# The square root of the pre-norm: a first guess by ACT's logarithm and exponential and one Newton step on DVE, for an integer guess and three steps

## The chip, the cores and the metric

The kernel runs on one core of a Trainium2 chip. The metric is the device time of one execution in microseconds (us); the time of before is the median of three runs. TensorE is called PE in the rows, VectorE DVE, ScalarE ACT, GpSimd POOL and SyncE SP.

## The reference

One inference step of a two-layer decoder, for a prompt of 512 tokens and 8 samples of 4 tokens each (544 tokens in all, 1024 features). Each layer has three sublayers, so there are six: feed-forward, mixer, feed-forward, twice. The mixer of the first layer is attention with a short convolution (A/B), that of the second a gated delta rule (C). Every sublayer starts with a norm of its input:

```python
def rmsnorm(x, g):
    xf = x.astype(jnp.float32)
    y = xf * lax.rsqrt(jnp.mean(xf * xf, axis=-1, keepdims=True) + NORM_EPS)
    return (y * g.astype(jnp.float32)).astype(x.dtype)

def swiglu(x, w_gate, w_up, w_down):
    return (jax.nn.silu(x @ w_gate) * (x @ w_up)) @ w_down

for layer in range(DEPTH):
    x = x + 0.5 * rmsnorm(swiglu(rmsnorm(x, gains[0]), ...), gains[1])
    x = x + rmsnorm(mixer(rmsnorm(x, gains[2]), ...), gains[3])
    x = x + 0.5 * rmsnorm(swiglu(rmsnorm(x, gains[4]), ...), gains[5])
```

## The kernel before

Activations lie with features on the partitions and the 544 tokens in columns, in two halves of 272. Every product is made in three passes: weights and activations are each split into a high and a low part, and high by high, high by low and low by high are summed. A **unit** is one block of weights, 128 output features by 1024 (or 1408) inputs, and costs TensorE 48 (or 66) matmuls. For each unit SP loads the raw weights (w_raw, a ring of four), ACT casts them to the high part (w_hi, L440, `act_split`), DVE subtracts to get the low part (w_lo, L447, `dve_split`), and TensorE multiplies (L455 or L467). w_hi and w_lo have two places each, so the cast for unit n + 2 waits until unit n is done.

Each engine has its own program, written out by hand; semaphores alone order them. There is no scheduler: what stands earlier in an engine's code runs earlier.

The norm ahead of a sublayer is folded behind its products. The products run on gain * x, and each result is multiplied by one factor per token, 1 / sqrt(mean + eps), when it is taken from PSUM. TensorE sums the squares over the features in the head of the sublayer (`pe_head`, L481), together with the first two units. DVE (`dve_rstd_x`, L843) writes the mean to a scratch tile, makes the low part of the third unit, and then takes the root into rb, which is called rstd_rows in the rows. `dve_rsqrt` does it by an integer guess of two operations and three Newton steps of three operations, each waiting for the last. Only then can DVE evict the first result, and only behind that eviction does it make the low part of the fourth unit:

```python
            if opening and j == 0:
                dve_rstd_x(e, s, n + 2)
            e.wait_ge(sem("unit_done"), i * 4 + (n + 1))
            if j % 2 == 0:
                e.tensor_tensor(halves(scr[:, m % 2, :]), cols(4 * (m % 2)), halves(rb[:, :]), ...
```

`dve_rsqrt` is also used for the norms behind the sublayers (on 3 columns) and inside mixer C; these stay. The six roots meant here belong to gate_up00, the A/B mixer, gate_up01, gate_up10, the C mixer and gate_up11, in this order. In mixer C, DVE waits for constants that POOL makes (L1746, the last) before it uses the root.

ACT's functions come from tables that are loaded in sets. Before, ACT loads the set with Silu at the head of each gate_up and of mixer C, and the set with logarithm and exponential at the head of mixer A/B and later in mixer C. Copies and squares run with either set.

Of the kernel before, what the change touches and what calls it, by code (L numbers as in the profile page):

```python
# [103 lines left out]
def build(nc, io, subs=SUBLAYERS):  # L104

    stack = ExitStack()
    with stack:
        sems = {}

        def sem(name):  # L110
            if name not in sems:
                sems[name] = stack.enter_context(nc.semaphore(name))
            return sems[name]
# [229 lines left out]
        gemms = {}  # L343
# [49 lines left out]
        def nk_of(n):  # L393
            for name in order:
                g = gemms[name]
                if g["n0"] <= n < g["end"]:
                    return g["nk"]
            return 0
# [33 lines left out]
        def act_split(e, n, i, nk):  # L432

            if not nk:
                return
            e.wait_ge(sem(f"w_raw{n % RAW}"), i * 16 + 16 * (n // RAW + 1))
            if n >= 2:

                e.wait_ge(sem("unit_done"), i * 4 + (n - 1))
            e.copy(w_hi[:, n % 2, 0:nk * P], raw[:, n % RAW, 0:nk * P]).then_inc(sem("w_hi_ready"), 1)  # L440
# [78 lines left out]
        def quads(e, g, body, peel):  # L519

            n = g["quads"] - (1 if peel else 0)
            with e.Fori(0, n) as i:
                body(i, False)
            if peel:
                body(g["quads"] - 1, True)
# [22 lines left out]
            with e.Fori(1, g["quads"]) as i:  # L548
                body(i, 0)

        def act_gate_up(e, g):
            m0 = gate_up_count(g)
            e.preload_act_table(ACT.Silu)

            def body(i, last):
                for j in range(4):
                    n = g["first"] + j
                    act_split(e, n + 2, i, nk_of(n + 2 + 4 * (g["quads"] - 1)) if last else KD)
                    if j % 2:
                        m = m0 + j // 2  # L560
                        e.wait_ge(sem("gate_scaled"), i * 2 + (m + 1))
                        e.activation(scr[:, m % 2, :], scr[:, m % 2, :], ACT.Silu).then_inc(sem("silu_ready"), 1)
                        e.wait_ge(sem("hidden_ready"), PRIMED + i * 2 + (m + 1))
                        e.copy(h_hi[:, bass.ds(i * 2 + j // 2, 1), :],  # L564
                               scr[:, 2 + m % 2:3 + m % 2, :]).then_inc(sem("h_hi_ready"), 1)

            quads(e, g, body, True)

        def dve_gate_up(e, g, s):
            m0 = gate_up_count(g)  # L570
# [158 lines left out]
        def act_y(e, g, y, s, pre):  # L729
            per, n_end = per_quad(g), g["first"] + 4 * (g["quads"] - 1)  # L730
            name = g["name"]

            def whole(i, j):
                n = g["first"] + j
                act_split(e, n + 2, i, g["nk"])
                if per == 4 or j % 2:
                    t = j // 2 if per == 2 else j
                    e.wait_ge(sem("unit_done"), i * 4 + (n + 1))
                    e.copy(y[:, bass.ds(i * per + t, 1), :].rearrange("p o (h t) -> p (o h) t", h=2), cols(2 * (t % 2)))
                    if isinstance(i, int) and i == 0 and t == 0:  # L740
                        to = scr[:, 2, :]
                    else:
                        to = scr[:, t % 2, :]
                        if not (isinstance(i, int) and i * per + t < 3):
                            e.wait_ge(sem("y_accumulated"), i * per + (acc_base[name] + t - 2))
                    e.activation(halves(to), cols(2 * (t % 2)), ACT.Square).then_inc(sem("y_squared"), 1)

            def tail(h):
                for m in tails_of(g):
                    if h == 0 and m >= 3 and per == 2:  # L750
                        e.wait_ge(sem("y_accumulated"), acc_base[name] + m - 2)
                    if h == 0 and per == 4:
                        e.wait_ge(sem("y_accumulated"), acc_base[name] + min(m - 2, KD - 3))
                    bank = 2 * (m % 2) + h
                    e.activation(scr[:, m % 2, half(h)], ps[:, bank, 0:TH], ACT.Square).then_inc(sem("y_squared"), 1)
                for m in tails_of(g):
                    ins = e.copy(y[:, m, half(h)], ps[:, 2 * (m % 2) + h, 0:TH])
                ins.then_inc(sem("tail_out"), 1)

            for j in range(4):  # L760
                whole(0, j)
            if g["quads"] > 2:
                with e.Fori(1, g["quads"] - 1) as i:
                    for j in range(4):
                        whole(i, j)
            for j in range(2):
                whole(g["quads"] - 1, j)
            e.wait_ge(sem("tail_done"), s + 1)
            tail(0)
            act_split(e, n_end + 4, 0, nk_of(n_end + 4))  # L770
            if pre:
                act_pre(e, s + 1, 0, 0, 2)
            e.wait_ge(sem("unit_done"), n_end + 4)
            tail(1)
            act_split(e, n_end + 5, 0, nk_of(n_end + 5))
            if pre:
                act_pre(e, s + 1, 0, 2, KD)
                act_pre(e, s + 1, 1, 0, KD)
# [41 lines left out]
        def dve_rsqrt(e, out, tmp, x):  # L820

            chain(e, e.tensor_scalar(tmp.bitcast(I32), x.bitcast(I32), 1, None, ALU.arith_shift_right))
            chain(e, e.tensor_scalar(out.bitcast(I32), tmp.bitcast(I32), -1, MAGIC, ALU.mult, ALU.add))
            for _ in range(3):
                chain(e, e.tensor_tensor(tmp, out, out, ALU.mult))
                chain(e, e.scalar_tensor_tensor(tmp, tmp, -0.5, x, ALU.mult, ALU.mult))
                chain(e, e.scalar_tensor_tensor(out, tmp, 1.5, out, ALU.add, ALU.mult))
# [15 lines left out]
        def dve_rstd_x(e, s, n):  # L843

            e.wait_ge(sem("squares_summed"), 2 * KD * (s + 1))
            mean, tmp = scr[:, 2, :], scr[:, 3, :]
            e.tensor_scalar(halves(mean), cols(4), 1.0 / D_MODEL, EPS, ALU.mult, ALU.add).then_inc(sem("mean_ready"), 1)
            dve_split(e, n, 0, KD)
            e.wait_ge(sem("mean_ready"), s + 1)
            dve_rsqrt(e, rb[:, :], tmp, mean)  # L850

        def gain(l, n, k):
            at = (l * 6 + n) * KD + k
# [501 lines left out]
        def act_ab(e, at):  # L1355
            g = gemms["ab_qkv"]
            e.preload_act_table_set("natural_log_exp_and_others")
            act_split(e, g["n0"] + 2, 0, KD)
            for u in range(11):
                act_split(e, g["first"] + u + 2, 0, KD)  # L1360
                if u == 1:
                    e.wait_ge(sem("vector_stage"), nth["gate_abs"])
                    e.activation(scr[0:A_HEADS, 1, :], scr[0:A_HEADS, 1, :], ACT.Exp
                                 ).then_inc(sem("scalar_stage"), reached("gate_exp"))
                if u == 2:
                    e.wait_ge(sem("vector_stage"), nth["gate_exp1"])
                    e.activation(scr[0:A_HEADS, 3, :], scr[0:A_HEADS, 2, :], ACT.Ln
                                 ).then_inc(sem("scalar_stage"), reached("gate_log"))
# [879 lines left out]
            return ext(m)[:, CP:CW].rearrange("p (b t) -> p b t", t=CS)  # L2248

        def act_c(e, at):  # L2250
            e.preload_act_table(ACT.Silu)

            g = gemms["c_qkv"]

            def raw_out(i, j):
# [26 lines left out]
                        silu_out(i, j - 1)  # L2282

            act_split(e, g["n0"] + 2, 0, KD)
            body(0, True, False)
            with e.Fori(1, g["quads"] - 1) as i:
                body(i, False, False)
# [564 lines left out]
        @block.scalar  # L2852
        def _(e):
            act_split(e, 0, 0, KD)
            e.wait_ge(sem("vector_stage"), nth["gains_ready"])
            act_pre(e, 0, 0, 0, KD)
            act_split(e, 1, 0, KD)
            act_pre(e, 0, 1, 0, KD)
            for s, (kind, l, w) in enumerate(subs):
                if kind == "ffn":  # L2860
                    act_gate_up(e, gemms[f"gate_up{l}{w}"])
                    act_y(e, gemms[f"down{l}{w}"], y_ffn, s, s + 1 < len(subs))
                if kind == "ab":
                    act_ab(e, s)
                if kind == "c":
                    act_c(e, s)
            for u in (0, 1, 2, 3, 4, 6):
                e.wait_ge(sem("rows_psum"), u + 1)
                e.copy(rows_p[:, u // 2, 4 * (u % 2) * P:4 * (u % 2 + 1) * P], ps[:, u % 4, :]).then_inc(sem("rows_out"), 1)
            e.wait_ge(sem("rows_psum"), 2 * PT + 1)  # L2870
            e.copy(rows_s[:, :].rearrange("p (a n) -> p a n", a=2), ps[0:NS, 4:6, :]).then_inc(sem("rows_out"), 1)
# [72 lines left out]
```

## Time and profile before

| | |
|---|---|
| median of three runs | 2992.24 us (2991.02 to 2996.61) |
| profiled execution | 2995.98 us |
| its span | 2992.8 us |
| TensorE busy | 2787.0 us, 93% |
| DVE busy | 1336.5 us, 45% |
| ACT busy | 845.8 us, 28% |
| mean granted clock of TensorE | 0.944 |

The table is read so: the span is from the first to the last instruction of the profiled execution, and the shares are of that span. An engine that is busy for less than half of it can still make TensorE wait, at the places where its work is needed next.

### The profile page before, as it was taken

The numbers are of one execution on the slowest core, as the hardware profiler recorded it, in microseconds if no ns is written. First come the engines' busy times: TensorE is split into PE (matmuls) and PEld (weight loads), VectorE is DVE, ScalarE is ACT, GpSimd is POOL, SyncE is SP. The second block draws the span as 40 slices with busy tenths as digits, with TensorE's granted clock in tenths as the row PEclk, the third lists the DMA queues.
The fourth block names the chain that finished last, engine by engine and source line by source line (L and its number), as shares of the span: only waits on it lengthen the run. The fifth ranks groups of instructions, "written<-read, shape, count | busy, mean of one in ns | idle before, by whom it ended". The sixth has DMA issues, their size and how long they took to land.

```text
span 2992.8 us, 52614 instructions
## 1 busy us (share of the span) xinstructions
PE 2787.0 (93%) x20906; PEld 2593.5 (87%) x20906; DVE 1336.5 (45%) x2270; ACT 845.8 (28%) x1409; POOL 359.0 (12%) x522
## 2 busy tenths in 40 slices
PE   7999999997887999999999999899999767999998
PEld 6999999875553899999899999899999536899998
DVE  5444236554442354432544422775365343644423
ACT  3222222233221332222322222443332212322222
POOL 0000012001232000000100000652343000100001
PEclk9999999998988899999999999999899657999999
DMA  3233322315786122332132332232100203232331
GB/s 108 85 90 95 93 67 78 80 36 171 259 273 217 57 71 85 91 99 85 51 91 84 96 98 67 62 89 59 34 1 1 64 29 85 59 90 84 103 90 41
DMA packets 404837, 263.01 MB, mean 88 GB/s; under 512 B 10954, under 2 KB 378775, under 8 KB 404665
## 3 DMA queue, kind: packets, MB, share of 16 engines
q1 hardware_dynamic: 394332, 227.22, 26.1%
q0 software_dynamic: 10384, 34.09, 3.5%
q8 instruction: 87, 1.43, 0.2%
q14 instruction: 34, 0.28, 0.0%
HBM read 251.71 MB, written 9.56 MB: 87 GB/s over the span
## 4 chain that ended last, share of the span: by engine, by line
PE 63%; DVE 6%; issue 2%; ACT 2%; DMA 1%; POOL 1%; SPq 1%; POOLq 0%; DVEq 0%; ACTq 0%
PE ps L467 45%; PE ps L455 3%; PE ps L2083 1%; PE ps L2100 1%; DMA k_pages<-in_cache_a_k_dram 1%; PE ps L1252 1%; PE ps L2098 1%; PE ps L2033 1%; PE ps L1274 1%; PE ps L1319 1%; PE ps L1984 1%; PE ps L1267 1%; PE ps L2220 1%; DVE states L2757 1%; PE ps L2067 1%
## 5 line engine op out<-in xcount | busy, mean ns | idle before, releaser
L447 DVE TENSOR_TENSOR w_lo<-w_raw,w_hi 128x1024 fp32r<-128x1024 f32 (+1 forms) x314 | 419.5, 1336 | 983.8 <-ACT w_hi L440 982.5
L467 PE MATMUL ps<-hd_hi,w_hi 128*128 128x272 f32 x3744 | 784.4, 291 | 30.4 <-DVE w_lo L447 20.9
L467 PE MATMUL ps<-hd_hi,w_lo 128*128 128x272 f32 x3744 | 779.2, 290 | 0.0
L467 PE MATMUL ps<-hd_lo,w_hi 128*128 128x272 f32 x3744 | 776.2, 289 | 0.0
L440 ACT CAST w_hi<-w_raw 128x1024 fp32r<-128x1024 f32 (+1 forms) x314 | 350.2, 1115 | 1096.1 <-PE ps L467 1044.7
L467 PEld LDWEIGHTS ps<-hd_hi,w_hi 128*128 128x128 f32 x3744 | 593.1, 190 | 38.2 <-issue 15.4
L467 PEld LDWEIGHTS ps<-hd_lo,w_hi 128*128 128x128 f32 x3744 | 592.7, 190 | 0.0
L467 PEld LDWEIGHTS ps<-hd_hi,w_lo 128*128 128x128 f32 x3744 | 589.1, 190 | 0.0
L882 POOL TENSOR_TENSOR xT<-xT,rstd_rows 128x272 f32<-128x272 f32 x96 | 81.5, 877 | 1855.7 <-DVE rstd_rows L907 1855.7
L467 PE MATMUL ps<-h_hi,w_lo 128*128 128x272 f32 x1232 | 255.0, 288 | 0.0
L467 PE MATMUL ps<-h_hi,w_hi 128*128 128x272 f32 x1232 | 254.7, 288 | 0.0
L467 PE MATMUL ps<-h_lo,w_hi 128*128 128x272 f32 x1232 | 253.9, 288 | 0.0
L467 PEld LDWEIGHTS ps<-h_hi,w_hi 128*128 128x128 f32 x1232 | 193.7, 188 | 0.0
L467 PEld LDWEIGHTS ps<-h_lo,w_hi 128*128 128x128 f32 x1232 | 193.6, 189 | 0.0
L467 PEld LDWEIGHTS ps<-h_hi,w_lo 128*128 128x128 f32 x1232 | 192.3, 189 | 0.0
L1252 PE MATMUL ps<-ident,k_pages 128*128 128x128 f32 x512 | 90.1, 328 | 36.4 <-DVE k_turned L1645 10.8
L1252 PEld LDWEIGHTS ps<-ident,k_pages 128*128 128x128 f32 x512 | 70.4, 170 | 59.1 <-issue 47.0
L564 ACT CAST h_hi<-scratch 128x544 f32 (+1 forms) x88 | 57.0, 648 | 201.7 <-DVE scratch L592 201.7
L455 PE MATMUL ps<-hd_hi,w_hi 128*128 128x272 f32 x256 | 94.9, 371 | 5.7 <-DVE hd_lo L860 4.6
L595 DVE TENSOR_TENSOR h_lo<-scratch,h_hi 128x544 f32 (+1 forms) x88 | 63.9, 726 | 79.7 <-ACT h_hi L564 79.7
L1049 POOL DMA_DIRECT2D v_pages<-in_cache_a_v_dram x128 | 69.0, 539 | 189.1 <-PE ps L1319 105.8
L1645 DVE COPY k_turned<-ps 128x512 f32<-128x512 f32 x64 | 44.3, 692 | 74.9 <-PE ps L1252 74.6
(496 smaller groups left out, 3303.0 us busy)
## 6 DMA issues: line engine op xcount, KB each, us to landing
w_raw<-in_ffn_w_gate_dram SPq DMA_DIRECT2D x88, 512.0 KB, 3.8
w_raw<-in_ffn_w_up_dram SPq DMA_DIRECT2D x88, 512.0 KB, 3.8
w_raw<-in_ffn_w_down_dram SPq DMA_DIRECT2D x64, 704.0 KB, 4.6
k_pages<-in_cache_a_k_dram SPq DMA_DIRECT2D x128, 256.0 KB, 4.8
v_pages<-in_cache_a_v_dram POOLq DMA_DIRECT2D x128, 256.0 KB, 4.9
w_raw<-in_c_w_in_dram SPq DMA_DIRECT2D x33, 512.0 KB, 4.1
w_raw<-in_ab_w_in_dram SPq DMA_DIRECT2D x25, 512.0 KB, 4.0
w_raw<-in_ab_w_out_dram SPq DMA_DIRECT2D x8, 512.0 KB, 3.9
```

What stands on the lines that cost most here:

```text
L440: e.copy(w_hi[:, n % 2, 0:nk * P], raw[:, n % RAW, 0:nk * P]).then_inc(sem("w_hi_ready"), 1)
L447: e.tensor_tensor(w_lo[:, n % 2, 0:nk * P], raw[:, n % RAW, 0:nk * P], w_hi[:, n % 2, 0:nk * P].bitcast(F32), ALU.subtract).then_inc(sem(" ...
L455: mm = e.matmul(ps[:, bank + h, 0:TH], w, x[:, kx, half(h)], start=first and w is wh and x is x_hi, stop=last and w is wl)
L467: mm = e.matmul(ps[:, bank + h, 0:TH], w, x[:, k0 + k, half(h)], start=first and k == 0 and w is wh and x is x_hi, stop=last and k == nk - ...
L564: e.copy(h_hi[:, bass.ds(i * 2 + j // 2, 1), :], scr[:, 2 + m % 2:3 + m % 2, :]).then_inc(sem("h_hi_ready"), 1)
L595: e.tensor_tensor(h_lo[:, bass.ds(i * 2 + j // 2, 1), :], scr[:, 2 + m % 2:3 + m % 2, :], h_hi[:, bass.ds(i * 2 + j // 2, 1), :].bitcast(F32),
L882: e.tensor_tensor(xT[:, k, half(h)], xT[:, k, half(h)], rb[:, half(k % 2)], ALU.add).then_inc(sem("x_ready"), 1)
L1049: e.dma_start(v_page[:, g, :].rearrange("p (o n) -> p o n", o=1), v_cache[:, bass.ds(page, 1), :]).then_inc(sem(f"v_page{g // 4}"), 16)
L1252: mm = e.transpose(ps[:, g % 2, q * P:(q + 1) * P], k_page[:, KR - 1 - g % KR, q * P:(q + 1) * P], ident[:, :])
L1267: mm = e.matmul(ps[q * NS:(q + 1) * NS, 2 + 4 * (G % 2), :], q_now[:, q * 40:q * 40 + NS], k_turned[:, G % 2, q, :], start=True, stop=True)
L1274: mm = e.matmul(ps[:, 7, at:at + NS], s_rows[:, G % 2, x * PAGE:(x + 1) * PAGE], pick[:, :], start=True, stop=True)
L1645: e.tensor_copy(k_turned[:, G % 2, :, (g % GP) * PAGE:(g % GP + 1) * PAGE], ps[:, 1, :].rearrange("p (q n) -> p q n", n=PAGE)).then_inc(se ...
```

## The change

The root's first guess moves to ACT: exp(-0.5 * ln(mean)), two operations over 128 partitions and 544 columns. DVE waits for it and does one Newton step. The two ACT operations need the set with logarithm and exponential. So in a feed-forward sublayer Silu's set is loaded behind them, and the other set again at the start of the down product, where another sublayer follows. ACT's loop over the quads of units has its first round written out, since the root stands inside it.

```diff
+        def act_root(e, s):
+
+            e.wait_ge(sem("mean_ready"), s + 1)
+            e.activation(rb[:, :], scr[:, 2, :], ACT.Ln).then_inc(sem("root_seed"), 1)
+            e.wait_ge(sem("root_seed"), 2 * s + 1)
+            e.activation(rb[:, :], rb[:, :], ACT.Exp, scale=-0.5).then_inc(sem("root_seed"), 1)
+
-        def act_gate_up(e, g):
+        def act_gate_up(e, g, s):
             m0 = gate_up_count(g)
-            e.preload_act_table(ACT.Silu)
-
-            def body(i, last):
+            if s == 0:
+                e.preload_act_table_set("natural_log_exp_and_others")
+
+            def body(i, last, opening=False):
                 for j in range(4):
                     n = g["first"] + j
                     act_split(e, n + 2, i, nk_of(n + 2 + 4 * (g["quads"] - 1)) if last else KD)
+                    if opening and j == 0:
+                        act_root(e, s)
+                        e.preload_act_table(ACT.Silu)
                     if j % 2:
...
-            quads(e, g, body, True)
+            body(0, False, True)
+            with e.Fori(1, g["quads"] - 1) as i:
+                body(i, False)
+            body(g["quads"] - 1, True)
...
         def act_y(e, g, y, s, pre):
             per, n_end = per_quad(g), g["first"] + 4 * (g["quads"] - 1)
             name = g["name"]
+            if g["kind"] == "down" and pre:
+                e.preload_act_table_set("natural_log_exp_and_others")
...
             dve_split(e, n, 0, KD)
             e.wait_ge(sem("mean_ready"), s + 1)
-            dve_rsqrt(e, rb[:, :], tmp, mean)
+            e.wait_ge(sem("root_seed"), 2 * s + 2)
+            chain(e, e.tensor_tensor(tmp, rb[:, :], rb[:, :], ALU.mult))
+            chain(e, e.scalar_tensor_tensor(tmp, tmp, -0.5, mean, ALU.mult, ALU.mult))
+            chain(e, e.scalar_tensor_tensor(rb[:, :], tmp, 1.5, rb[:, :], ALU.add, ALU.mult))
...
             e.preload_act_table_set("natural_log_exp_and_others")
             act_split(e, g["n0"] + 2, 0, KD)
+            act_root(e, at)
...
         def act_c(e, at):
-            e.preload_act_table(ACT.Silu)
-
...
             act_split(e, g["n0"] + 2, 0, KD)
+            act_root(e, at)
+            e.preload_act_table(ACT.Silu)
             body(0, True, False)
```

How DVE's instructions stand at the head of gate_up01, the third root, from the low part of the third unit (w_lo) to that of the fourth. Before:

```order
L447 TENSOR_TENSOR w_lo<-w_raw,w_hi 128x1024
L822 TENSOR_SCALAR scratch<-scratch 128x544
L823 TENSOR_SCALAR rstd_rows<-scratch 128x544
L825 TENSOR_TENSOR scratch<-rstd_rows 128x544
L826 SCALAR_TENSOR_TENSOR scratch<-scratch 128x544
L827 SCALAR_TENSOR_TENSOR rstd_rows<-scratch,rstd_rows 128x544
...
L582 TENSOR_TENSOR scratch<-ps,rstd_rows 128x544
L447 TENSOR_TENSOR w_lo<-w_raw,w_hi 128x1024
```

Of the change, at the same place:

```order
L447 TENSOR_TENSOR w_lo<-w_raw,w_hi 128x1024
L867 TENSOR_TENSOR scratch<-rstd_rows 128x544
L868 SCALAR_TENSOR_TENSOR scratch<-scratch 128x544
L869 SCALAR_TENSOR_TENSOR rstd_rows<-scratch,rstd_rows 128x544
L596 TENSOR_TENSOR scratch<-ps,rstd_rows 128x544
L447 TENSOR_TENSOR w_lo<-w_raw,w_hi 128x1024
```

Eleven operations between the two low parts become three (the six rows left out repeat the Newton step twice); the eviction of the gate's result (L582, now L596) still stands behind them.

ACT at the same head, from the last square of the head (L874) to the first Silu (L562). Before:

```order
L874 ACTIVATE scratch<-xT 128x272
L553 ACT_TABLE_LOAD
L522 UNCONDITIONAL_BRANCH
L522 ISA
L439 ISA
L440 CAST w_hi<-w_raw 128x1024
L436 REGISTER_ALU
L439 REGISTER_ALU
L440 CAST w_hi<-w_raw 128x1024
L561 ISA
L562 ACTIVATE scratch<-scratch 128x544
```

Of the change:

```order
L893 ACTIVATE scratch<-xT 128x272
L440 CAST w_hi<-w_raw 128x1024
L554 ACTIVATE rstd_rows<-scratch 128x544
L556 ACTIVATE rstd_rows<-rstd_rows 128x544
L569 ACT_TABLE_LOAD
L440 CAST w_hi<-w_raw 128x1024
L573 ACTIVATE scratch<-scratch 128x544
```

The table load moves from ahead of the third unit's cast to ahead of the fourth's, with the logarithm (L554) and the exponential (L556) in front of it.

## Rows read from the trace of the kernel before

**Rows 1.** The page's busy line of TensorE (busy time, share, instructions).
```profile
PE 2787.0 (93%) x20906; PEld 2593.5 (87%) x20906; DVE 1336.5 (45%) x2270; ACT 845.8 (28%) x1409; POOL 359.0 (12%) x522
```

**Rows 2.** Waits, whole run: engine and line, its releaser, total us, times, longest.
```profile
PE ps L467 <- DVE w_lo L447: 20.9, 7, 5.7
```

**Rows 3.** Timeline of DVE at gate_up01's head: start, duration, instruction, idle before.
```profile
1059.45 0.72 DVE L847 TENSOR_SCALAR scratch<-ps 128x544 f32<-128x544 f32 x1 [1.24 <-PE ps L481]
1060.52 1.23 DVE L447 TENSOR_TENSOR w_lo<-w_raw,w_hi 128x1024 fp32r<-128x1024 f32 x1 [0.34 <-ACT w_hi L440]
1061.66 0.44 DVE L822 TENSOR_SCALAR scratch<-scratch 128x544 int32<-128x544 int32 x1
...
1068.69 0.72 DVE L827 SCALAR_TENSOR_TENSOR rstd_rows<-scratch,rstd_rows 128x544 f32<-128x544 f32 x1
...
1070.09 1.22 DVE L447 TENSOR_TENSOR w_lo<-w_raw,w_hi 128x1024 fp32r<-128x1024 f32 x1
```

**Rows 4.** Timeline of ACT over the same stretch.
```profile
1058.14 1.28 ACT L553 ACT_TABLE_LOAD   x1
1059.43 1.05 ACT L440 CAST w_hi<-w_raw 128x1024 fp32r<-128x1024 f32 x1
1062.45 1.06 ACT L440 CAST w_hi<-w_raw 128x1024 fp32r<-128x1024 f32 x1 [1.97 <-PE ps L455]
```

**Rows 5.** Timeline of PE, the first matmul behind each root.
```profile
55.06 0.52 PE L467 MATMUL ps<-hd_hi,w_hi 128*128 128x272 f32 x2 [2.95 <-DVE w_lo L447]
...
472.98 0.49 PE L467 MATMUL ps<-hd_hi,w_hi 128*128 128x272 f32 x2 [3.08 <-DVE w_lo L447]
...
1071.36 0.82 PE L467 MATMUL ps<-hd_hi,w_hi 128*128 128x272 f32 x2 [2.94 <-DVE w_lo L447]
...
1490.30 0.52 PE L467 MATMUL ps<-hd_hi,w_hi 128*128 128x272 f32 x2 [2.91 <-DVE w_lo L447]
...
1914.51 0.79 PE L467 MATMUL ps<-hd_hi,w_hi 128*128 128x272 f32 x2 [5.75 <-DVE w_lo L447]
...
2587.46 0.82 PE L467 MATMUL ps<-hd_hi,w_hi 128*128 128x272 f32 x2 [2.94 <-DVE w_lo L447]
```

**Rows 6.** Windows of 7 us from those matmuls: length, busy us, PEclk, DMA share.
```profile
55.06:62.06 7.00, 7.00 (x56) 7.00 (x56) 3.89 (x5) 2.27 (x3) 0.00 (x0) 1.00 0.41 122
472.98:479.98 7.00, 7.00 (x44) 7.00 (x45) 3.81 (x6) 0.66 (x1) 0.00 (x0) 0.76 0.56 152
1071.36:1078.36 7.00, 7.00 (x45) 7.00 (x46) 3.89 (x5) 1.59 (x2) 0.00 (x0) 0.79 0.41 119
1490.30:1497.30 7.00, 7.00 (x43) 7.00 (x44) 3.90 (x5) 1.59 (x2) 0.00 (x0) 0.76 0.39 115
1914.51:1921.51 7.00, 7.00 (x45) 7.00 (x46) 4.38 (x6) 1.08 (x5) 4.08 (x9) 0.79 0.88 225
2587.46:2594.46 7.00, 7.00 (x35) 7.00 (x36) 3.90 (x5) 1.59 (x2) 0.00 (x0) 0.58 0.41 120
```

**Rows 7.** Lines: group, out<-in, xcount, busy us, mean ns of one.
```profile
L825 DVE TENSOR_TENSOR scratch<-rstd_rows 128x544 f32<-128x544 f32 x18 | 13.1, 725 | 0.6
...
L553 ACT ACT_TABLE_LOAD x4 | 5.1, 1283 | 0.1
...
L1363 ACT ACTIVATE scratch<-scratch 8x544 f32<-8x544 f32 x1 | 0.7, 658 | 5.9 <-DVE scratch L1481 5.9
```

**Rows 8.** Timeline of DVE, then of POOL, at mixer C's head.
```profile
1912.16 0.72 DVE L2438 TENSOR_TENSOR ba_by_feature<-ps,rstd_rows 128x544 f32<-128x544 f32 x1 [1.60 <-POOL c_small L1746]
...
1901.38 2.03 POOL L1713 TENSOR_SCALAR_AFFINE_SELECT half_masks<-half_masks 128x128 f32<-128x128 f32 x2
...
1908.73 1.23 POOL L1713 TENSOR_SCALAR_AFFINE_SELECT half_masks<-half_masks 128x128 f32<-128x128 f32 x2
...
1911.93 0.10 POOL L1746 MEMSET c_small<- 128x1 f32 x1
```

**Rows 9.** Timeline of ACT, first cast of down01 that waits for TensorE.
```profile
1327.86 1.37 ACT L440 CAST w_hi<-w_raw 128x1408 fp32r<-128x1408 f32 x1 [3.09 <-PE ps L467]
```

More of the change, by code:

```diff
@@ L2860, in _ @@
                 if kind == "ffn":
-                    act_gate_up(e, gemms[f"gate_up{l}{w}"])
+                    act_gate_up(e, gemms[f"gate_up{l}{w}"], s)
                     act_y(e, gemms[f"down{l}{w}"], y_ffn, s, s + 1 < len(subs))
```

## The prediction

> **What bounds the kernel now.** Start with the page: TensorE is busy for 93% of the span, DVE for 45% and ACT for 28% [rows 1]. So a faster root on DVE is worth only what TensorE waits for it. Next come the waits: a weight product at L467 waited for a low weight part (L447, DVE) seven times, 20.9 us in all, 5.7 us at the longest [rows 2]. TensorE's timeline puts six of the seven right behind the six roots: 2.95, 3.08, 2.94, 2.91, 5.75 and 2.94 us [rows 5]. They make 20.57 us, and the rest is one wait of 0.4 us.
>
> Then the cause, read on DVE at the head of gate_up01, the third root [rows 3]. The mean is written from 1059.45 to 1060.17. The low part of the third unit follows from 1060.52 to 1061.75. The root starts at 1061.66 and its last Newton step ends at 1069.41. Behind it in DVE's order stand one eviction and the low part of the fourth unit, which starts at 1070.09 and ends at 1071.31; TensorE goes on at 1071.36, after 2.94 us of nothing. It had therefore ended the third unit at 1068.42. ACT is no part of this: its cast for the fourth unit is over at 1063.51 [rows 4].
>
> Last, the windows of granted clock from each restart, 7 us long: 1.00, 0.76, 0.79, 0.76, 0.79 and 0.58, with TensorE busy throughout [rows 6]. Where the mean is below 1.00 the clock stood at 1.2 GHz for part of the window and at 2.4 for the rest, after the idle stretch. A window at mean clock c loses 7 x (1 - c) us: 0, 1.68, 1.47, 1.68, 1.47 and 2.94 us.
>
> **The change part by part.** *Removed from DVE:* two integer operations and six of nine Newton operations per root, all 544 columns wide. *Added to ACT:* a logarithm and an exponential per root, each 544 columns wide. The nearest row is an exponential over 8 partitions and 544 columns, 0.66 us [rows 7]; the duration goes with the columns, and I take 0.66 us for each, with 0.05 us from one to the other. Bounds: 0.5 and 1.0 us each.
>
> At gate_up01 the new order runs so. ACT's cast of the third unit ends at 1060.48 [rows 4], later than the mean (1060.17), so the logarithm runs from 1060.52 to 1061.18 and the exponential from 1061.23 to 1061.89. DVE has ended its low part at 1061.75 and waits 0.2 us. Three operations of 0.725 us [rows 7] with 0.035 us between them end at 1064.2, against 1069.41 now: 5.2 us sooner. ACT then loads Silu's table, 1.283 us [rows 7], to 1063.2, and casts the fourth unit to 1064.25. That is before DVE's eviction is over, so the low part runs from 1064.9 to 1066.1. TensorE asks for it at 1068.42. It is 2.3 us early, and the whole 2.94 us stall goes. The other three gate_up heads have the same rows within 0.04 us [rows 5]. The mixer A/B head has the right table loaded already and needs no Silu behind the root, so it has more room. With either bound of the two ACT operations the low part ends between 1065.8 and 1066.8, still early.
>
> Five stalls: 2.95 + 3.08 + 2.94 + 2.91 + 2.94 = **14.82 us**.
>
> *The clock behind them.* Without the gap TensorE comes from one dense unit into the next. Now it runs at the upper clock where nothing interrupts it; behind the same gap it fell in four of these five cases. Losses of those five: 0 + 1.68 + 1.47 + 1.68 + 2.94 = **7.77 us** [rows 6]. The bounds are 0 (the falls come anyway, elsewhere) and 7.77; one of five gaps had no fall and another a double one, so the five look like a fair draw, and I take all of it. The Trainium skill speaks to this in "TensorE: Matmul & The Clock Gate", section "What's actually happening": the upper clock is held by sustained activity, and the number of slow matmuls changes from run to run of one kernel, so it should not be fitted. By its first half the sum is as mine; by its second only the 14.82 us should be counted. The trace agrees with both halves: no fall at 55.06 us, a fall at 1071.36 us, after gaps of the same length.
>
> *Mixer C.* There DVE does not go on at the root's end. After 1.60 us of idling it starts at 1912.16, released by POOL's last constant [rows 8], so the root now ends at about 1910.6. Ending it at 1905 instead only lengthens that wait. The 5.75 us stall and its slow clock stay. POOL can be faster by itself: a pair of mask operations took 2.03 us beside DVE's integer operations and a later pair, of another view, 1.23 us without them [rows 8]. Bounds for the gain: 0 and 0.8 us; I take **0.3 us**, nearer to nothing because the views differ.
>
> *Table loads.* ACT has four more: one behind the first root, and one at the start of each of three down products. The first lies in the slack worked out above. The others stand where ACT idles 3.09 us for TensorE before the first waiting cast of the down product [rows 9], so 1.28 us is hidden; were that cover gone, three times 1.28 us would be 3.8 us. The loads of the other gate_up heads only move from ahead of the third unit's cast to ahead of the fourth's. "ScalarE: Activation LUTs" in the Trainium skill, section "What ACT_TABLE_LOAD costs", speaks against the change: a switch of sets costs some 2.66 us, a drain included. The trace shows the load of 1.28 us ending at 1059.42 and the next cast starting at 1059.43, without a drain [rows 4]. By the page the fourth unit's low part would end near 1066.8 rather than 1066.1 and still be early, and the down loads would still fit into 3.09 us.
>
> *The sum.* 14.82 + 7.77 + 0.3 = 22.9 us. The profiled execution took 2995.98 us for a span of 2992.8; it would take 2973.1 us. It stands 3.7 us above the median of the three runs, 2992.24, and carries the same stalls, so the median becomes **2969.3 us**, 0.8% less.
>
> **The rivals.** *The clock gives nothing back.* The falls are drawn anew by the shifted times, at the sublayers' ends and in the decode part. For it: one gap in five had no fall. Against it: four did. Time: 2992.24 - 15.1 = 2977.1 us.
>
> *Part of the gain is absorbed later.* Between the A/B root and the end of its mixer TensorE waits for other things; if they do not move with it, the 3.08 + 1.68 us of that root are lost: 2974.1 us. Against it: that root's stall is on the same line as the others, and POOL's constants there would have to be late.
>
> *The change doesn't do what it says.* What keeps the fourth unit back would turn out to be the cast, because ACT now stands in the chain: peeled code that comes late, or ACT operations of over 1.8 us each instead of 0.66 (2.3 us of room, for two). If most of each stall stayed, 2989 us.
>
> *Slower.* One mechanism: the table loads are not 1.28 us in their new places but wait for their data. The cast of the fourth unit may end as late as 1070.09 before anything is worse than today, which leaves 1070.09 - 1064.25 = 5.8 us on top of 1.28. So it decides from a load of 7.1 us on. At 10 us each, four gate_up heads lose 2.9 us each, 11.6 in all, the A/B head still gains 4.8, and the time is 2999 us. The four loads ahead of the gate_up casts took 1.283 us in the mean [rows 7], so I hold this for remote.
>
> **How the numbers follow.** My forecast has a chance of 0.75, the clock's rival 0.12, the absorbed part 0.06, no effect 0.04, slower 0.03. About 0.2% (6 us) is what a measurement can tell from no change. The first three are beyond it: faster 0.93; same 0.04; slower 0.03. The range: below, mixer C's 0.5 us more and some three clock falls fewer than in the runs before (1.7 us each) give 2964 us; above, the clock's rival at 2977.1 us. I give 2963.5 to 2977.5 us.
>
> **What would show it.** Right: DVE's three operations behind a wait of about 0.2 us for ACT; no wait of TensorE for L447 behind five roots and the full clock there; at mixer C a DVE wait for POOL of 6 to 7 us in place of 1.6; the stall there near 5.5 us. Wrong: a cast of the fourth unit that starts after the gate's eviction, a gap behind a table load, a stall at the first casts of a down product, or new clock falls at the sublayers' ends that eat the 7.8 us.

## The result, and the profile after

The changed kernel takes 2972.85 us (median of six runs, 2966.37 to 2974.34); the kernel before, run beside it, 2995.34 us (six runs, median). The ratio is 0.991, with a 95% interval of 0.9884 to 0.9937: 0.9% faster, beyond the 0.2% that a measurement can tell. The profiled execution took 2968.84 us for a span of 2966.8, which is 26.0 us less of span than before. TensorE's busy time in it is 2782.4 us, where it was 2787.0 [rows 1], so of the 26.0 us 4.6 are busy time and 21.4 are idle time. In all comparisons together one execution of the kernel before took 3936.91 us at a granted clock of 0.637; no ratio here has it in.

In the waits of the changed kernel, TensorE's wait for a low weight part is down from seven times and 20.9 us [rows 2] to one of 3.8 us; DVE's wait for POOL at mixer C has grown to 5.2 us, where it was 1.60 [rows 8]:

```profile
PE ps L467 <- DVE w_lo L447: 3.8, 1, 3.8
...
DVE ba_by_feature L2458 <- POOL c_small L1766: 5.2, 1, 5.2
```

DVE's timeline at the head of gate_up01, the same place as [rows 3]:

```profile
1048.24 0.72 DVE L863 TENSOR_SCALAR scratch<-ps 128x544 f32<-128x544 f32 x1 [1.23 <-PE ps L481]
1048.92 1.23 DVE L447 TENSOR_TENSOR w_lo<-w_raw,w_hi 128x1024 fp32r<-128x1024 f32 x1
1050.46 0.72 DVE L867 TENSOR_TENSOR scratch<-rstd_rows 128x544 f32<-128x544 f32 x1 [0.31 <-ACT rstd_rows L556]
1051.21 0.72 DVE L868 SCALAR_TENSOR_TENSOR scratch<-scratch 128x544 f32<-128x544 f32 x1
1051.97 0.73 DVE L869 SCALAR_TENSOR_TENSOR rstd_rows<-scratch,rstd_rows 128x544 f32<-128x544 f32 x1
1052.73 0.72 DVE L596 TENSOR_TENSOR scratch<-ps,rstd_rows 128x544 f32<-128x544 f32 x1
1053.38 1.22 DVE L447 TENSOR_TENSOR w_lo<-w_raw,w_hi 128x1024 fp32r<-128x1024 f32 x1
```

Read it from the top: mean, low part of the third unit, a wait of 0.31 us for ACT's guess, one Newton step, the gate's eviction, and the low part of the fourth unit, over at 1054.60. From the mean's start to the start of that low part it is 5.14 us, where it was 10.64 [rows 3].

ACT over the same stretch:

```profile
1047.84 1.05 ACT L440 CAST w_hi<-w_raw 128x1024 fp32r<-128x1024 f32 x1 [0.93 <-PE ps L455]
1049.00 0.66 ACT L554 ACTIVATE rstd_rows<-scratch 128x544 f32<-128x544 f32 x1
1049.69 0.66 ACT L556 ACTIVATE rstd_rows<-rstd_rows 128x544 f32<-128x544 f32 x1
1050.37 1.28 ACT L569 ACT_TABLE_LOAD   x1
1051.66 1.05 ACT L440 CAST w_hi<-w_raw 128x1024 fp32r<-128x1024 f32 x1
...
1057.32 1.05 ACT L440 CAST w_hi<-w_raw 128x1024 fp32r<-128x1024 f32 x1 [0.58 <-PE ps L467]
```

The cast of the third unit is followed by logarithm, exponential and table load, and the cast of the fourth starts 0.01 us after the load's end, without a drain. The last row shows when TensorE was done with the third unit: at 1057.3. The low part of the fourth unit had been ready for 2.7 us (1054.60).

Windows of 7 us of the changed kernel, at the end of the third unit in five heads and behind the remaining gap at mixer C. The first window starts 2.6 us ahead of that end and the fourth 2.4 us behind it; windows laid at the ends, 52.60 and 1470.57, have a clock of 1.00 too. The columns are length, busy us of PE, PEld, DVE, ACT and POOL, granted clock, DMA share and GB/s:

```profile
50.00:57.00 7.00, 7.00 (x58) 7.00 (x58) 4.11 (x6) 1.70 (x2) 0.00 (x0) 1.00 0.34 97
467.40:474.40 7.00, 7.00 (x59) 7.00 (x57) 3.40 (x5) 2.58 (x3) 0.98 (x3) 1.00 0.48 139
1057.20:1064.20 7.00, 7.00 (x59) 7.00 (x58) 2.15 (x3) 1.92 (x2) 0.00 (x0) 1.00 0.33 98
1473.00:1480.00 7.00, 7.00 (x58) 7.00 (x57) 2.74 (x4) 1.61 (x2) 0.00 (x0) 1.00 0.26 77
1889.68:1896.68 7.00, 7.00 (x37) 7.00 (x38) 4.38 (x6) 1.07 (x5) 4.08 (x9) 0.64 0.90 225
2565.00:2572.00 7.00, 7.00 (x58) 7.00 (x58) 2.23 (x3) 1.84 (x2) 0.00 (x0) 1.00 0.34 100
```

Five times the clock is 1.00 with TensorE busy throughout, where [rows 6] had 1.00, 0.76, 0.79, 0.76 and 0.58. Mixer C has 0.64.

The span cut at the mean of each root shows where the time came from. Before:

```profile
43.13:460.94 417.81, 411.03 (x3230) 407.00 (x3229) 172.16 (x226) 118.06 (x156) 15.77 (x24) 1.00 0.29 83
460.94:1059.45 598.51, 524.67 (x3607) 399.49 (x3606) 274.80 (x571) 164.33 (x323) 106.89 (x191) 0.91 0.46 146
1059.45:1478.41 418.96, 412.17 (x3230) 408.43 (x3229) 172.43 (x227) 118.00 (x156) 13.92 (x16) 0.99 0.29 83
1478.41:1900.51 422.10, 415.32 (x3262) 410.99 (x3261) 172.92 (x229) 119.20 (x156) 18.07 (x31) 0.99 0.29 82
1900.51:2575.56 675.05, 590.48 (x4279) 542.91 (x4278) 363.38 (x771) 202.74 (x459) 191.65 (x233) 0.86 0.18 47
2575.56:2992.80 417.24, 404.28 (x3164) 401.63 (x3162) 163.63 (x210) 105.61 (x127) 11.68 (x16) 0.98 0.27 81
```

After:

```profile
43.62:458.47 414.85, 410.92 (x3230) 407.11 (x3229) 166.74 (x218) 121.87 (x160) 15.76 (x24) 1.00 0.29 84
458.47:1048.24 589.77, 524.25 (x3607) 399.06 (x3606) 270.00 (x563) 164.66 (x324) 106.97 (x191) 0.90 0.46 149
1048.24:1461.59 413.35, 409.41 (x3230) 405.67 (x3229) 166.78 (x219) 120.67 (x159) 14.18 (x16) 1.00 0.29 84
1461.59:1877.60 416.01, 412.07 (x3262) 408.02 (x3260) 167.58 (x221) 121.28 (x159) 18.22 (x31) 1.00 0.29 83
1877.60:2556.12 678.52, 595.48 (x4279) 548.34 (x4278) 357.97 (x763) 204.54 (x461) 189.46 (x233) 0.85 0.17 47
2556.12:2966.80 410.68, 400.62 (x3164) 398.26 (x3162) 158.44 (x202) 107.90 (x130) 11.68 (x16) 0.99 0.28 82
```

The stretches changed by -3.0, -8.7, -5.6, -6.1, +3.5 and -6.6 us, and the piece ahead of the first by +0.5. The only one that grew is the fifth, mixer C's. The second column is TensorE's busy time; a slow clock lengthens it (in [rows 6] a window of 7 us with TensorE busy throughout holds 56 matmuls at a clock of 1.00 and 35 at 0.58), and a wait does not count in it.

### The profile page after: what moved, and what is told of

Its sections match the earlier page's. It is cut to its first block, busy times and chain, and to the rows that moved or that the text cites. A ratio compares the mean times of both kernels' runs of the same rounds, so it can differ in the third digit from the quotient of the medians.

```text
span 2966.8 us, 52549 instructions
## 1 busy us (share of the span) xinstructions
PE 2782.4 (94%) x20906; PEld 2590.1 (87%) x20906; DVE 1304.7 (44%) x2222; ACT 858.8 (29%) x1425; POOL 357.3 (12%) x522
## 4 chain that ended last, share of the span: by engine, by line
PE 65%; DVE 5%; ACT 2%; issue 2%; POOL 1%; DMA 1%; SPq 0%; POOLq 0%; DVEq 0%; ACTq 0%
PE ps L467 46%; PE ps L455 3%; PE ps L1271 2%; PE ps L2103 1%; PE ps L2120 1%; PE ps L2118 1%; PE ps L2053 1%; PE ps L1293 1%; PE ps L1286 1%; PE ps L1338 1%; DMA k_pages<-in_cache_a_k_dram 1%; PE ps L2004 1%; PE ps L481 1%; DVE states L2777 1%; PE ps L2087 0%
```

## The experiments

Each kernel ran beside the kernel before on the same chip; the ratio is to that kernel, with its 95% interval. The first four experiments share one set of runs of the kernel before (2994.78 us), the last four another (2993.39 us).

**Three Newton steps behind the guess**:

```diff
-            chain(e, e.tensor_tensor(tmp, rb[:, :], rb[:, :], ALU.mult))
...
+            for _ in range(3):
+                chain(e, e.tensor_tensor(tmp, rb[:, :], rb[:, :], ALU.mult))
...
```

> The changed kernel with three Newton steps instead of one behind ACT's first guess. My theory: TensorE waits only for what the root's chain exceeds its room. In the changed kernel the fourth unit's low part is 2.7 us early at gate_up01; two more steps are 6 operations of 0.76 us, 4.6 us, so five heads wait 1.9 us each (9.4 us), partly with a clock fall of up to 1.7 us each: 10 to 16 us more than the changed kernel, 6 to 12 us less than before. Rival (every microsecond taken from DVE's root counts, room or not): two steps at six roots cost 27 us, so slower than before by about 1 us. At mixer C POOL's mask pairs should go back from about 0.7 to 1.2 us if DVE's Newton operations hinder them, and stay at 0.7 if only the removed integer operations did.

Measured: 2987.72 us (ten runs) against 2994.78, ratio 0.9981 [0.9964, 0.9999]; that is 14.9 us more than the changed kernel's 2972.85. TensorE's gaps behind the five roots are 2.17, 2.25, 1.99, 1.99 and 1.99 us; the third of them and mixer C's:

```profile
1067.24 0.52 PE L467 MATMUL ps<-hd_hi,w_hi 128*128 128x272 f32 x2 [1.99 <-DVE w_lo L447]
...
1906.72 0.79 PE L467 MATMUL ps<-hd_hi,w_hi 128*128 128x272 f32 x2 [5.34 <-DVE w_lo L447]
```

The two added steps take 4.6 us. Of these the changed kernel has room for 2.7 us; 1.9 us are left over, and the rows say 1.99. The interval reaches up to almost no change, so the time alone hardly refutes the rival; the gaps, and the next run, do.

**Two Newton steps**, by the same edit with range(2).

> The changed kernel with two Newton steps. My theory: 2.3 us later than with one step, within the room of 2.7 us, so no wait of TensorE behind the five roots; only mixer C's gap is longer by up to 1 us. Time within 0.1% of the changed kernel, 19 to 25 us less than before. Rival (every microsecond counts): 13.7 us more than the changed kernel, some 9 us less than before.

Measured: 2970.57 us (four runs), ratio 0.9926 [0.9898, 0.9954], the same as the changed kernel within the scatter. TensorE waits for a low part once, at mixer C:

```profile
PE ps L467 <- DVE w_lo L447: 4.4, 1, 4.4
```

A second step adds 12.7 us to DVE's busy time (1317.4 us against 1304.7) and nothing behind the five roots. What counts is the chain less its room, not DVE's work. The rival, which had only 9 us less than before where 24 were measured, is out.

**The order alone: the kernel before, with the low part of the fourth unit behind the first of its three steps.**

```diff
         def dve_rsqrt(e, out, tmp, x, between=None):
             for _ in range(3):
...
+                if between is not None:
+                    dve_split(e, between, 0, KD)
+                    between = None
...
-            dve_rsqrt(e, rb[:, :], tmp, mean)
+            dve_rsqrt(e, rb[:, :], tmp, mean, n + 1)
```

(and the three loops behind the heads leave that low part out).

> The kernel before, root wholly on DVE with integer guess and three steps, but the low part of the fourth unit stands behind the first Newton step rather than behind the root and the eviction. My theory (TensorE waits for that low part alone): the gaps behind all six roots go, mixer C's too since its low part no longer stands behind the wait for POOL: 20.6 us of gaps and up to 9.2 us of slow clock, 20 to 30 us less than before, no worse than the changed kernel. Rival (the evictions behind the root are needed just as early): the gap moves to the fifth unit or later, and under 10 us are gained.

Measured: 2977.87 us (six runs), ratio 0.9949 [0.9931, 0.9968]: 17 us less, short of the 20 expected and more than the 10 that the rival allowed. Neither theory had it whole. The gap behind the A/B root is gone. In the four feed-forward heads it moved one unit on and shrank to 1.4 us. At mixer C it moved on and grew to 7.6 us:

```profile
1068.57 0.52 PE L467 MATMUL ps<-hd_hi,w_hi 128*128 128x272 f32 x2 [1.39 <-DVE w_lo L447]
...
1907.43 0.79 PE L467 MATMUL ps<-hd_hi,w_hi 128*128 128x272 f32 x2 [7.61 <-DVE w_lo L447]
```

DVE's timeline at gate_up01 of this kernel, from the end of the root, says why:

```profile
1063.35 0.73 DVE L582 TENSOR_TENSOR scratch<-ps,rstd_rows 128x544 f32<-128x544 f32 x1
1063.99 0.71 DVE L588 TENSOR_TENSOR scratch<-ps,rstd_rows 128x544 f32<-128x544 f32 x1
1064.81 0.73 DVE L592 TENSOR_TENSOR scratch<-scratch 128x544 f32<-128x544 f32 x1
1066.34 0.72 DVE L595 TENSOR_TENSOR h_lo<-scratch,h_hi 128x544 fp32r<-128x544 f32 x1 [0.81 <-ACT h_hi L564]
1067.29 1.22 DVE L447 TENSOR_TENSOR w_lo<-w_raw,w_hi 128x1024 fp32r<-128x1024 f32 x1 [0.23 <-ACT w_hi L440]
```

The gate's and the up's eviction, the product and h_lo stand ahead of the fifth unit's low part, and all of them need the root. So the late root reaches TensorE through the evictions too, a unit later.

**The table loads alone: the kernel before with the loads where the change has them, and the first round of ACT's loop written out.** Nothing else of the change is in it.

```diff
                     act_split(e, n + 2, i, nk_of(...) if last else KD)
+                    if opening and j == 0:
+                        e.preload_act_table(ACT.Silu)
...
+            if g["kind"] == "down" and pre:
+                e.preload_act_table_set("natural_log_exp_and_others")
```

> The kernel before with the table loads of the changed kernel (four more, five others moved behind the third unit's cast), no logarithm or exponential, root as before. My theory: all loads lie in ACT's idle time, no change beyond 0.1%, TensorE's waits behind the roots within 0.1 us of before. Rival (a switch costs the page's 2.66 us where it stands ahead of a cast): the cast of the fourth unit is still early, but four more loads lengthen ACT's path by 10.6 us in all; 0.2 to 0.4% slower if any of it is exposed.

Measured: 2994.93 us (ten runs) against 2994.78, ratio 0.9994 [0.9984, 1.0004]: the added loads cost nothing. Three of the gaps are even 0.4 us shorter, as at gate_up01:

```profile
1072.95 0.52 PE L467 MATMUL ps<-hd_hi,w_hi 128*128 128x272 f32 x2 [2.54 <-DVE w_lo L447]
```

There the load no longer stands ahead of the third unit's cast, so that cast, and DVE's root behind it, come earlier. The gain of the change at these three heads has this small part in it, which the expectation ("within 0.1 us") had missed.

**The changed kernel again**, as the base for the next three.

> The changed kernel itself once more, as the base for the three others on the same chip. Expected 20 to 26 us less than before, no wait of TensorE behind five roots, 3.8 us at mixer C.

Measured: 2967.56 us (four runs) against 2993.39, ratio 0.9916 [0.989, 0.9942], 25.8 us less; the gap at mixer C is 3.83 us again.

**POOL's half masks later:** in the changed kernel the loop that makes the seven mask levels moves behind POOL's convolution loop of mixer C.

```diff
-            for l in range(LEVELS):
...
             chained(e.memset(c_small[:, :], 0.0))
             e.memset(c_small[:, 500:501], 0.0).then_inc(sem("gpsimd_stage"), reached("c_constants_ready"))
...
                 for j in range(4):
                     pool_ext(e, i, j)
+            for l in range(LEVELS):
...
```

> The changed kernel with POOL making mixer C's half masks behind its convolution loop, not ahead of it, so that the constants DVE waits for are ready some 10 us earlier. My theory (in the changed kernel mixer C's gap is set by POOL alone): DVE evicts right behind the Newton step, the gap of 3.83 us goes but for some 0.6 us at the next unit, and with it the slow clock behind it (about 2.3 us): 4 to 6 us less than the changed kernel. Rival (the first unit's convolution on DVE and POOL is the bound and the gap only moves by a unit): under 2 us less.

Measured: 2964.21 us (five runs), ratio 0.9898 [0.9882, 0.9915]; 3.4 us less than the changed kernel on the same chip, a little short of the 4 to 6 expected, and a difference that the scatter of single runs does not quite resolve. The rows do: DVE evicts right behind the Newton step, and the gap at the fourth unit is gone.

```profile
1880.72 0.73 DVE L869 SCALAR_TENSOR_TENSOR rstd_rows<-scratch,rstd_rows 128x544 f32<-128x544 f32 x1
1881.48 0.72 DVE L2458 TENSOR_TENSOR ba_by_feature<-ps,rstd_rows 128x544 f32<-128x544 f32 x1
...
1882.46 1.22 DVE L447 TENSOR_TENSOR w_lo<-w_raw,w_hi 128x1024 fp32r<-128x1024 f32 x1 [0.23 <-DVE scratch L2460]
```

All waits of TensorE for low parts in that kernel:

```profile
PE ps L467 <- DVE w_lo L447: 0.7, 2, 0.5
```

At the next unit, where 0.6 us were expected, TensorE waits 0.21 us (at 1891.49). The other wait, 0.53 us, stands at 2030.55, late in mixer C's projections.

**The same move in the kernel before.**

> The kernel before with the same move of the half masks. There the root ended 1.6 us ahead of POOL's last constant, so the root becomes the bound at once: the gap at mixer C shrinks from 5.75 to 4.1 us, somewhat less if the root is no longer slowed by POOL. Time 1 to 3 us less than before. Rival (POOL's masks set the gap in both kernels alike): the gap goes as in the changed kernel with this move.

Measured: 2992.69 us (ten runs) against 2993.39, ratio 0.9995 [0.9979, 1.0012], no change that can be told; the 1 to 3 us expected would have been too small for it. The gap shrank from 5.75 to 3.65 us, somewhat more than to the 4.1 forecast, and did not go:

```profile
1911.53 0.79 PE L467 MATMUL ps<-hd_hi,w_hi 128*128 128x272 f32 x2 [3.65 <-DVE w_lo L447]
```

With POOL out of the way the long root is the bound there. The two edits need each other: either alone leaves 3.7 to 3.8 us of gap, both together leave 0.21 us.

**The low part of mixer C's fourth unit ahead of DVE's wait for POOL**, in the changed kernel.

```diff
                 dve_rstd_x(e, s, g["n0"] + 2)
+                dve_split(e, g["n0"] + 3, 0, KD)
```

(and the loop behind it leaves that low part out).

> The changed kernel with the low part of mixer C's fourth unit ahead of DVE's wait for POOL. My theory, after the order experiment: the gap leaves the fourth unit and comes back at the fifth, whose low part stands behind the first convolution; 0 to 2 us less than the changed kernel. Rival (the low part alone matters there): the gap of 3.8 us and its slow clock go, 5 to 6 us less.

Measured: 2971.02 us (four runs), ratio 0.9931 [0.9907, 0.9955]: no less than the changed kernel, where 0 to 2 us less were expected. The gap left the fourth unit and came back at the fifth, longer:

```profile
1900.61 0.79 PE L467 MATMUL ps<-hd_hi,w_hi 128*128 128x272 f32 x2 [5.38 <-DVE w_lo L447]
```

So at mixer C, too, the evictions and what follows from them set the pace; an earlier low part only moves the gap.

## Why the prediction was right, and where it was off

**Five gaps, 14.82 us.** Right, and by the step it named. All five are gone, the low part of the fourth unit comes 2.7 us before TensorE asks (2.3 forecast), and two_steps and three_steps show the room from both sides. Most of the 0.4 us more comes from the table load that no longer delays the third unit's cast: DVE had idled 0.34 us for that cast [rows 3] and does so no more. ACT's operations took the 0.66 us assumed.

**The clock behind them, 7.77 us.** Right in the windows, five of them at 1.00; over the whole execution TensorE's busy time fell by 4.6 us, not by 7.77. The forecast took the five losses for a fair draw. The clock fell behind four of five gaps of 2.9 to 3.1 us before, behind four of five in tables_only (2.5 to 3.1 us) and four of five in before_masks_late (2.9 to 3.1 us); behind one of five gaps of 2.0 to 2.3 us in three_steps; behind none of four gaps of 1.4 us in order_only. TensorE's busy time says the same: 2787.0, 2794.9 and 2788.2 us in the three kernels with five gaps of 2.5 to 3.1 us, and 2779.3 to 2782.4 in the five kernels without a gap behind those roots (the changed kernel twice, two_steps, masks_late and c_early). So the gain is there on average, and shortening a gap saves more than its own length. That gaps draw the falls is shown by these counts; the size in one execution is chance. Nothing in this kernel was run that keeps the gaps and prevents the falls, so the 7.77 us were not measured apart.

**Mixer C, 0.3 us.** The mechanism was right (DVE waits for POOL's last constant), the term was mis-sized: the gap shrank from 5.75 to 3.83 us, 1.9 us, outside the bounds of 0 to 0.8, and DVE waited 5.2 us for POOL, not 6 to 7. The forecast laid POOL's slowness to DVE's integer operations. Its pair of 2.03 us, from 1901.38 to 1903.41, ran beside the third unit's low part (to 1902.36) as well as the integer operations, and that low part stays; the same pair takes 2.42 us in the changed kernel, beside the low part, ACT's two operations and the first Newton operation. Most of what the change gives back comes from the Newton operations. POOL's fourteen mask operations (line, count, busy us and mean ns of one), before:

```profile
L1713 POOL TENSOR_SCALAR_AFFINE_SELECT half_masks<-half_masks 128x128 f32<-128x128 f32 x14 | 9.1, 651 | 1.0
```

In the changed kernel, with one step:

```profile
L1733 POOL TENSOR_SCALAR_AFFINE_SELECT half_masks<-half_masks 128x128 f32<-128x128 f32 x14 | 7.4, 526 | 1.0
```

With two steps, and with three, behind ACT's guess:

```profile
L1734 POOL TENSOR_SCALAR_AFFINE_SELECT half_masks<-half_masks 128x128 f32<-128x128 f32 x14 | 7.9, 567 | 1.0
```

```profile
L1734 POOL TENSOR_SCALAR_AFFINE_SELECT half_masks<-half_masks 128x128 f32<-128x128 f32 x14 | 8.9, 635 | 1.0
```

Three steps without any integer operation already bring back 8.9 of the 9.1 us. TensorE's gap there goes with it: 5.75 us before, 5.34, 4.38 and 3.83 with three, two and one steps behind ACT's guess. So moving the first guess to ACT gives 0.4 us, and each Newton step that DVE leaves out 0.6 to 1.0 us.

**The stretch of mixer C grew all the same,** by 3.5 us, with 1.9 us less of gap at its head. TensorE's busy time in it rose by 5.0 us. Part is the draw of the clock: 0.64 in the window behind the gap (a loss of 2.5 us) against 0.79 before (1.5 us). The rest stands in the chunk steps, whose code is the same: three of them took 139.97 us before and 144.00 us after, with granted clocks of 1.00, 1.00 and 0.93 before and 0.97, 0.96 and 0.91 after. The kernel before with only POOL's masks moved took 678.1 us for this stretch, as much as the changed kernel, so its length moves by some 3 us without the root.

**The A/B mixer gained 8.7 us for 4.8 forecast,** and this is no draw of the clock: TensorE's busy time in that stretch is the same (524.67 and 524.25 us), so what was won behind the gap was lost again elsewhere in it. Its idle time fell by 8.3 us. The gap is 3.08 of them, and TensorE's waits for the loads of the cached keys and values are 5.1 (those for the values went from 13.8 to 12.5 us). For the keys, before:

```profile
PE ps L1252 <- DMA k_pages<-in_cache_a_k_dram: 9.5, 8, 2.2
```

After:

```profile
PE ps L1271 <- DMA k_pages<-in_cache_a_k_dram: 5.7, 6, 1.6
```

It is no accident of one execution either: the stretch took 597.7 to 599.1 us in the three kernels with the full gap and 589.3 to 592.5 in the six without it. No experiment varied these loads; why TensorE waits less for them stays open.

**The sum.** The median fell by 22.5 us for a forecast of 22.9, but the terms did not all come as forecast, and that they met so closely is in part luck. In the profiled execution idle time gave 21.4 us where 15.1 were forecast (14.82 from the five gaps, 1.9 from mixer C, the rest, 4.7, is about what the waits for the A/B mixer's loads lost) and the clock 4.6 where 7.77 were.

**Table loads.** Hidden, as costed: tables_only shows no cost, and the first waiting cast of down01 still idles behind its load:

```profile
1309.35 1.28 ACT L747 ACT_TABLE_LOAD   x1
1312.13 1.37 ACT L440 CAST w_hi<-w_raw 128x1408 fp32r<-128x1408 f32 x1 [1.49 <-PE ps L467]
```

The idle time is 1.49 us where it was 3.09 [rows 9]. The Trainium skill's drain behind a switch of sets ("ScalarE: Activation LUTs", section "What ACT_TABLE_LOAD costs") does not appear in any row here: casts follow 0.01 us behind the loads at the heads.

**The rivals.** The windows alone do not refute that the clock gives nothing back, since the falls could come elsewhere; TensorE's busy times above do, and so does the time: this rival had 15.1 us less, and the least that the interval allows is 18.9 (2995.34 x 0.0063). That part of the gain is absorbed in the A/B mixer holds for the clock's 1.68 us only; as a whole its stretch gained most. No effect and slower needed late casts; the cast of the fourth unit ended at 1052.71, ahead of its turn on DVE.

## What to carry to other kernels

A chain on an engine that is busy for 45% of the time can still stop TensorE once per stage; what it costs is its length less the room that TensorE's present unit gives, so shorten it only to that point (here a second Newton step was free). Before making a chain faster, look at what its engine waits for at the end of it: at mixer C it was another engine's constants, and a move of these was worth as much there as the faster root (each alone took about 2 us off the gap, both together all but 0.21 us; alone, the move of the constants could not be told in the time). Moving the waited-for operation ahead of the chain is not the same as shortening the chain, since everything else behind it is late as well and the gap comes back a unit later.

## What the hardware showed that was not expected

POOL and DVE hinder each other on SBUF work. The sixth pair of POOL's mask operations, the same code and the same view, took 1.22 us in three_steps, beside Newton operations of 128x544 fp32, and 0.66 us in the changed kernel, with DVE idle:

```profile
1901.13 1.22 POOL L1734 TENSOR_SCALAR_AFFINE_SELECT half_masks<-half_masks 128x128 f32<-128x128 f32 x2
...
1884.65 0.66 POOL L1733 TENSOR_SCALAR_AFFINE_SELECT half_masks<-half_masks 128x128 f32<-128x128 f32 x2
```

In the other direction the kernel before shows it: DVE's two integer operations took 0.77 and 0.63 us at mixer C, where POOL was at work, and 0.44 and 0.45 us at gate_up01, where it was idle. DVE's Newton operations beside POOL took 0.72 to 0.77 us, hardly longer than elsewhere (0.72).

Gaps of TensorE do not cost alike by length: of fifteen gaps of 2.5 to 3.1 us twelve were followed by a time at 1.2 GHz, of nine gaps of 1.4 to 2.3 us one. All nine long gaps at mixer C, 3.65 to 7.61 us, were followed by one.
